# The first stage reordered: modulation by column groups, input weights in four transfers, half of the projection begun behind the first group

## The reference

```python
def rms_norm(x, g):
    return x * rsqrt(mean(x*x, -1) + 1e-6) * g
def modulate(x, g, shift, scale):
    return rms_norm(x, g) * (1 + scale) + shift

m  = silu(c)     @ w_mod + b_mod          # [1, 6*1024]; w_mod is [1024, 6144]
mc = silu(c_ctx) @ w_mod + b_mod
sh1, sc1, g1, sh2, sc2, g2 = split(m, 6)  # columns 0:1024 shift, 1024:2048 scale, ...
hx = modulate(x,   norm_attn_pre, sh1, sc1)
hc = modulate(ctx, norm_attn_pre, csh1, csc1)   # from mc
px = hx @ w_in                            # w_in is [1024, 960]
pc = hc @ w_in
# then: latent norms, query/key/value projections, rotation, attention of x over x and ctx,
# a Fourier mixing of part of px, w_out, the gated residual with g1,
# and a mixture of 32 experts, 4 for each token, over modulate(x, norm_ffn_pre, sh2, sc2).
# The second block (two layers of other attention kinds, each with an MLP) follows.
```

## Time and profile before

| | us |
|---|---|
| median of 3 runs | 1879.67 |
| lowest, highest | 1878.62, 1880.48 |
| span of the profiled execution, from first to last instruction | 1877.3 |

### The profile page before, as it was taken

How to read it: one execution, slowest core, us unless ns; L and a number is a source line. 1 busy time by engine, 2 the same in 40 slices (tenths; PEclk the granted TensorE clock), 3 DMA queues, 4 the chain that set the end, 5 groups by cost and what they waited for, 6 DMA issues and landing times. The chain is left out here.

```text
span 1877.3 us, 21793 instructions
## 1 busy us (share of the span) xinstructions
PE 1824.7 (97%) x8661; PEld 998.6 (53%) x8662; DVE 505.1 (27%) x1093; ACT 348.3 (19%) x688; POOL 10.9 (1%) x14
## 2 busy tenths in 40 slices
PE   6999899999999999999999999999999999999998
PEld 5757533333333333333333336768885466788743
DVE  1754411111011111011111104542025443211355
ACT  3221411111111111111111113332000032220001
POOL 0000000000000000000000000000000000000001
PEclk9999899999999999999999999999999999999999
DMA  9986599999999999999999999423355443134252
GB/s 401 324 184 276 207 416 430 431 432 432 431 431 431 433 431 431 431 431 432 431 431 430 432 429 328 155 105 105 135 176 177 146 174 135 45 135 158 86 170 102
DMA packets 101218, 558.43 MB, mean 297 GB/s; under 512 B 16936, under 2 KB 33805, under 8 KB 74413
## 3 DMA queue, kind: packets, MB, share of 16 engines
q1 hardware_dynamic: 98612, 553.06, 72.4%
q10 hardware_dynamic: 2554, 4.63, 1.9%
HBM read 552.43 MB, written 5.23 MB: 297 GB/s over the span
## 5 line engine op out<-in xcount | busy, mean ns | idle before, releaser
L1362 PE MATMUL ps<-ring,xs 128*64 128x512 f32 x2112 | 466.9, 593 | 8.5 <-DMA ring<-in_w_up 4.7
L1362 PEld LDWEIGHTS ps<-ring,xs 128*64 128x64 f32 x2112 | 151.1, 137 | 312.7 <-issue 293.9
L1416 PE MATMUL ps<-ring,actT 128*64 128x512 f32 x1056 | 233.9, 595 | 0.0
L2149 PE MATMUL ps<-hT,ring 128*128 128x256 f32 x1024 | 222.0, 379 | 0.2 <-ACT hT L1614 0.2
L2149 PEld LDWEIGHTS ps<-hT,ring 128*128 128x128 f32 x1024 | 194.3, 190 | 27.0 <-ACT hT L1614 0.6
L2174 PE MATMUL ps<-ring 128*128 128x512 f32 x448 | 192.8, 592 | 0.0
L1416 PEld LDWEIGHTS ps<-ring,actT 128*64 128x64 f32 x1056 | 73.1, 137 | 158.5 <-issue 131.7
L1489 DVE TENSOR_SCALAR hT<-ps 128x512 f32<-128x512 f32 x33 | 22.8, 692 | 448.0 <-PE ps L1362 448.0
L2174 PEld LDWEIGHTS ps<-ring 128*128 128x128 f32 x448 | 85.0, 190 | 105.8 <-issue 105.7
L1937 PE MATMUL ps<-hT,ring 128*128 128x256 f32 x512 | 117.9, 383 | 4.3 <-ACT hT L1614 2.9
L1937 PEld LDWEIGHTS ps<-hT,ring 128*128 128x128 f32 x512 | 94.7, 190 | 23.2 <-issue 5.9
(11 more groups left out here) (434 smaller groups left out, 1548.1 us busy)
## 6 DMA issues: line engine op xcount, KB each, us to landing
ring<-in_w_up SPq DMA_DIRECT2D x64, 2048.0 KB, 23.2
ring<-in_w_down SPq DMA_DIRECT2D x64, 2048.0 KB, 24.2
ring<-in_w_gate SPq DMA_DIRECT2D x64, 2048.0 KB, 22.7
ring<-in_mlp_w SPq DMA_DIRECT2D x16, 2048.0 KB, 7.7
ring<-in_mlp_w SPq DMA_DIRECT2D x32, 1024.0 KB, 5.3
ring<-in_w_mod SPq DMA_DIRECT2D x8, 2048.0 KB, 15.4
ring<-in_odd_w_in SPq DMA_DIRECT2D x6, 2048.0 KB, 7.7
ring<-in_w_mod SPq DMA_DIRECT2D x8, 1024.0 KB, 14.1
```

The costliest lines, as they stand in the source:

```text
L1362: mm = pe.matmul(ps[SLOTS * half:SLOTS * (half + 1), bank, :], xs[:, c % 4, c // 4 * SLOTS:(c // 4 + 1) * SLOTS], weights(v, 8 * part + c) ...
L1416: mm = pe.matmul(ps[SLOTS * half:SLOTS * (half + 1), Y, :], actT[:, f % 4, f // 4 * SLOTS:(f // 4 + 1) * SLOTS], weights(v, 16 + f)[:, hal ...
L2149: mm = pe.matmul(ps[:, bank + f // 2, (f % 2) * SEQ:(f % 2 + 1) * SEQ], mlp_w1[layer][g % 2][:, c, f * P:(f + 1) * P], hT[:, c, :], start= ...
```

## The change

- The first part of `w_mod` is split by column group: group g holds columns 512g to 512g+511 of shift and of scale. Each group is loaded by eight transfers (a chunk each, half a MiB, rows of 2 KB), into ring rows 0 to 7 and 8 to 15.
- `w_in` is loaded in four quarters, two behind each group's transfers.
- TensorE turns x first, into banks 4 to 7, then the small vectors, then `xn` into banks 0 to 3, now also behind `cols_ready`. The modulation runs group by group: four strips of 256 columns. Group 0 comes ahead of the projection, group 1 in the midst of it: its matmuls ahead of chunk 3's products, its transposes behind four of these.
- VectorE adds the bias and makes the gain for each group, chunks 0 to 3 for group 0, 4 to 7 for group 1, and so makes its four `hT` chunks behind group 1. ScalarE copies each group's bank on its own.
- SyncE's wait ahead of the second parts, and GpSimd's ahead of the clearing of `acc`, are for the second group now.

The diff, cut to its core:

```diff
+    moda = [ring[:, 8 * g:8 * g + 8, :].rearrange("p c (s n) -> p c s n", s=2) for g in range(2)]
...
-    win_in = [m.sem(f"win_in{k}") for k in range(2)]
+    win_in = [m.sem(f"win_in{k}") for k in range(4)]
...
-            pool.wait_ge(mods_ps, 1)
+            pool.wait_ge(mods_ps, 2)
             pool.memset(acc, 0.0).then_inc(zeroed, 1)
...
             sp.dma_start(x[:], stack(t["x"][0])).then_inc(x_in, 16)
-            for c in range(C):
-                sp.dma_start(ring[:, 2 * c:2 * c + 2, :].rearrange("p a n -> p (a n)"),
-                             t["w_mod"][0, c * P:(c + 1) * P, 0:2 * D]).then_inc(moda_in[c], 16)
-            for i in range(2):
-                src = stack(t["w_in"][0, 512 * i:512 * i + 512, :])
-                sp.dma_start(win[:, 4 * i:4 * i + 4, 0:IN_W], src).then_inc(win_in[i], 16)
-                sp.dma_start(win[:, 4 * i:4 * i + 4, IN_W:D], src[:, :, IN_W - ROPE:IN_W]).then_inc(win_in[i], 16)
+            halves = t["w_mod"][0].rearrange("(c p) (s n) -> p c s n", p=P, n=D)
+            for g in range(2):
+                for q in range(4):
+                    for k in range(2):
+                        c = 2 * q + k
+                        sp.dma_start(moda[g][:, c, :, :], halves[:, c, 0:2, 512 * g:512 * g + 512]).then_inc(moda_in[4 * g + q], 16)
+                for q in (2 * g, 2 * g + 1):
+                    src = stack(t["w_in"][0, 256 * q:256 * q + 256, :])
+                    sp.dma_start(win[:, 2 * q:2 * q + 2, 0:IN_W], src).then_inc(win_in[q], 16)
+                    sp.dma_start(win[:, 2 * q:2 * q + 2, IN_W:D], src[:, :, IN_W - ROPE:IN_W]).then_inc(win_in[q], 16)
             sp.dma_start(ctx_sb, stack(t["ctx"][0])).then_inc(ctx_in, 16)
...
-            sp.wait_ge(moda_ps, 1)
+            sp.wait_ge(moda_ps, 2)
             for c in range(3):
                 second_part(c)
...
             pe.wait_ge(consts_in, 16)
+            pe.wait_ge(x_in, 16)
+            turned(x, 4)
             pe.wait_ge(rows_in, 16 * len(ROWS))
-            pe.transpose(ps[:, 7, 0:NROWS], rows[0:NROWS, :], ident[0:NROWS, 0:NROWS]).then_inc(rows_t, 1)
-            pe.wait_ge(x_in, 16)
-            turned(x, 0)
+            pe.transpose(ps[:, 0, 0:NROWS], rows[0:NROWS, :], ident[0:NROWS, 0:NROWS]).then_inc(rows_t, 1)
             pe.wait_ge(normed, QT)
+            pe.wait_ge(cols_ready, 1)
+            turned(xn, 0)
+
+            def modulation(g, bank):
+
+                for c in range(C):
+                    if c % 2 == 0:
+                        pe.wait_ge(moda_in[4 * g + c // 2], 32)
+                    for j in range(4):
+                        mm = pe.matmul(ps[32 * j:32 * (j + 1), bank, 0:SEQ], silu32[:, c, :],
+                                       moda[g][:, c, j // 2, (j % 2) * SEQ:(j % 2 + 1) * SEQ], start=(c == 0), stop=(c == C - 1))
+                mm.then_inc(mods_ps, 1)
+
+            def modulation_turned(g, bank):
+                pe.wait_ge(mods_sb, g + 1)
+                for b in range(2):
+                    mm = pe.transpose(ps[:, bank, b * P:(b + 1) * P], mods[:, g * SEQ + b * P:g * SEQ + (b + 1) * P], ident)
+                mm.then_inc(moda_ps, 1)
+
+            pe.wait_ge(silu_ready, 2)
             pe.wait_ge(copied_a, 2)
             pe.wait_ge(copied_v, 2)
-            turned(xn, 0)
-
-            pe.wait_ge(silu_ready, 2)
-            for c in range(C):
-                pe.wait_ge(moda_in[c], 16)
-                for j in range(4):
-                    mm = pe.matmul(ps[32 * j:32 * (j + 1), 5, :], silu32[:, c, :],
-                                   ring[:, 2 * c + j // 2, (j % 2) * 512:(j % 2 + 1) * 512], start=(c == 0), stop=(c == C - 1))
-            mm.then_inc(mods_ps, 1)
-            pe.wait_ge(mods_sb, 1)
-            pe.wait_ge(cols_ready, 1)
-            for b in range(4):
-                mm = pe.transpose(ps[:, 7, b * P:(b + 1) * P], mods[:, b * P:(b + 1) * P], ident)
-            mm.then_inc(moda_ps, 1)
+            modulation(0, 5)
+            modulation_turned(0, 7)
...
-            keep_busy(m, pe, 5, 6)
-            pe.wait_ge(modv_ready, 4)
+            keep_busy(m, pe, 5, 3)
+            pe.wait_ge(modv_ready, 2)
             for c in range(C):
...
-                if c % 4 == 0:
-                    pe.wait_ge(win_in[c // 4], 32)
+                if c % 2 == 0:
+                    pe.wait_ge(win_in[c // 2], 32)
+                if c == 3:
+                    modulation(1, 0)
...
                 for n in range(8):
+                    if c == 3 and n == 4:
+                        modulation_turned(1, 1)
                     mm = product(4 + n // 2, n % 2, c, AT[n], hT)
...
             act.wait_ge(mods_ps, 1)
-            act.copy(mods, ps[:, 5, :]).then_inc(mods_sb, 1)
+            act.copy(mods[:, 0:SEQ], ps[:, 5, 0:SEQ]).then_inc(mods_sb, 1)
...
             modulated(hT, 0, 0)
+            act.wait_ge(mods_ps, 2)
+            act.copy(mods[:, SEQ:2 * SEQ], ps[:, 0, 0:SEQ]).then_inc(mods_sb, 1)
             act.wait_ge(ctx_in, 16)
...
+            def modulation(g, bank):
+                v.wait_ge(moda_ps, g + 1)
+                v.wait_ge(cols_ready, 1)
+                parts = modv[:].rearrange("p (s g h b) t -> p s g h b t", s=2, g=2, h=2)
+                bias = col(m, "bmod", 0, 16).rearrange("p (s g h b a) -> p s g h b a", s=2, g=2, h=2, a=1)
+                for b in range(2):
+                    raw = ps[:, bank, b * P:(b + 1) * P].rearrange("p (s h t) -> p s h t", s=2, h=2)[:, :, :, 0:2]
+                    v.tensor_tensor(parts[:, :, g, :, b, :], raw, bias[:, :, g, :, b, :].to_broadcast([P, 2, 2, 2]), ALU.add).then_inc(modv_ready, 1)
+                v.wait_ge(modv_ready, 2 * g + 2)
+                v.scalar_tensor_tensor(gain[:, 4 * g:4 * g + 4, :], modv[:, 8 + 4 * g:12 + 4 * g, :], 1.0, spread(col(m, "pre", 4 * g, 4), 2),
+                                       ALU.add, ALU.mult).then_inc(gain_ready, 1)
+
+            modulation(0, 7)
...
-            v.wait_ge(gain_ready, 1)
+            modulation(1, 1)
+            v.wait_ge(gain_ready, 2)
             v.wait_ge(x_ps, 2)
             modulated(hT, 0, 0)
```

More of the change, by code:

```diff
@@ L771, in _ @@
             for k in range(2):
-                act.copy(xT[:, 2 * k:2 * k + 2, :].rearrange("p a n -> p (a n)"), ps[:, k, :]).then_inc(copied_a, 1)
+                act.copy(xT[:, 2 * k:2 * k + 2, :].rearrange("p a n -> p (a n)"), ps[:, 4 + k, :]).then_inc(copied_a, 1)
             act.wait_ge(cols_ready, 1)
@@ L807, in q @@
                 return latent(bank, half, qlatT[:, k, :], sq_q[:, k, :], col(m, "qlat", k))
+            act.wait_ge(gain_ready, 2)
             act.wait_ge(x_ps, 3)
@@ L949, in _ @@
             v.memset(m.eps[:, 1:2], EPS2).then_inc(m.init, 1)
-            v.wait_ge(rows_t, 1)
-            v.tensor_copy(m.cols[:], ps[:, 7, 0:NROWS]).then_inc(cols_ready, 1)
             def normalize(dst, src, j):
@@ L960, in _ @@
             normalize(xn, x, 0)
+            v.wait_ge(rows_t, 1)
+            v.tensor_copy(m.cols[:], ps[:, 0, 0:NROWS]).then_inc(cols_ready, 1)
             v.wait_ge(x_ps, 1)
             for k in range(2, 4):
[L963 to L971, removed]
+                v.tensor_copy(xT[:, 2 * k:2 * k + 2, :].rearrange("p a n -> p (a n)"), ps[:, 4 + k, :]).then_inc(copied_v, 1)
+            def modulation(g, bank):
[10 more added lines that the diff above has]
+            modulation(0, 7)
             def modulated(dst, bank, which):
```

## The result

The change makes the kernel slower by 4.2 us: 1883.66 us median (1882.40 to 1885.09, 15 runs) against 1879.47 (1877.02 to 1880.48, 15 runs) taken beside it, a ratio of 1.0024 with a 95% interval of 1.0017 to 1.0032. A second time, beside the experiments, it was 1883.29 against 1878.92: 1.0020, 1.0011 to 1.0030. The profiled execution's span went from 1877.3 to 1882.9.

A forecast was written before the change was run, and what follows sets the result against it. It took the transfer queue as first bound, then two nearly equal chains at 64 us: TensorE's, and second parts, b_mod, adds, hcT. Late flow 2.6 plus clock 1.7 gave +4.3, on 1879.67: 1884.0 us, range 1880.2 to 1888.0.

The forecast's parts named there:

- The shift passes to the end: From the expert passes on: a shift of the first stage moves products and transfers alike and passes undiminished to the end.
- Rival (e): Expert stage: expert loads keep their time and TensorE's 8.5 us of waits shrink by the shift; 1879.7 us, chance 0.08.
- TensorE's gain: x products: they begin at 22.1 instead of 32.41 and end at 55.7, 6.5 us earlier than before.
- rival (b): Modulation: group 0 runs at the low pace, 3.5 us more before the products; +7.8, 1887.5 us, chance 0.10.
- The second parts late: SyncE's queue: second parts wait for group 1 until 38.4, flow resumes at 40.3 against 37.7, 2.6 us later.
- GpSimd's clearing: Clearing of acc: moves to the second group (39.6) but ends before SyncE has issued its three second parts (3.46 us).
- b_mod in order: Transfer queue: b_mod keeps its place behind 6.3 MB of second parts and lands at 56.5, 2.6 us later.
- Rival (d): Transfer queue: b_mod doesn't queue, landing some 4 us after its issue at 42; -7.4, 1872.3 us, chance 0.08.
- The clock: Behind TensorE's 9 us idle gap before the context products: 3.4 us at half pace, 1.7 us lost.
- Rival (a): First stage: the clock stays up or TensorE comes 1 to 2 us earlier; +1.0 to +2.8, say 1881.5, chance 0.22.
- The small pieces: Modulation loads: 8.39 MB in 2 KB pieces run at 409 GB/s, costing 0.9 us.
- Rival (c): Modulation loads: half-size transfers are slow, 315 GB/s, and the queue never stands empty; 6.9 + 1.7, 1888.3 us, chance 0.04.

The follow-up runs named there:

- e1: The changed kernel with VectorE making its half of hcT ahead of the first eight modulation adds; 1872.58 us against 1878.88 for the kernel before.
- e4: The kernel before, with SyncE issuing the second parts only after TensorE's second chunk of x products; 1883.34 us against 1878.88.
- e10: The changed kernel itself timed once more, beside e11 on the same chip; 1883.29 us against 1878.92 for the kernel before.
- e11: The changed kernel with the edits of e2 and e3 together, 16 idle matmuls in the gap; 1880.31 us against 1878.92 for the kernel before.
- e2: The changed kernel with the first two second parts issued behind group 0's wait, not group 1's; 1881.72 us against 1878.88 for the kernel before.
- e3: The changed kernel with 19 idle matmuls in TensorE's gap ahead of the context's fifth chunk; 1882.12 us against 1878.88 for the kernel before.
- e9: e8 with VectorE's two copies out of the projection banks also ahead of the eight adds; 1874.34 us against 1878.46 for the kernel before.
- e5: The kernel before, with the first modulation part loaded in sixteen half-MiB transfers by column group; 1880.04 us against 1878.46.
- e8: e1 with the first two second parts issued behind group 0 and b_mod ahead of the third; 1871.57 us against 1878.46 for the kernel before.
- e6: The kernel before, with VectorE making its half of hcT ahead of the eight modulation adds; 1878.60 us against 1878.46.

## Why the prediction was right

The forecast was 1884.0, +4.3; measured were 1883.66, +4.2. The likeliest case came about by its mechanism. That the total fits so closely is in part luck: at the up projections, where the mechanism ends, the loss was 6.4 us, half as much again as forecast. By its steps:

- **The shift passes to the end.** Right: 1648.2 and 1648.5 us behind the first pass, and 1647.5 to 1648.2 in e1 to e4, e10 and e11. Rival (e) fell.
- **TensorE's gain.** Right in kind: 6.5 us were forecast; in the change itself it is 4.94 (57.29 for 62.23), and in e1, where nothing covers it, 6.07. The start of the products was 1.3 us late (23.39 for 22.1), since group 0 ran 4.77 us instead of 3.5. Group 1, at the later pace, took 3.66. In e2, e3 and e9 group 0 took 3.66 as well: the early part of the kernel meets the change of pace at different points. This is a small piece of rival (b).
- **The second parts late.** Right in mechanism, 1.2 us too small in size. Issued at 39.76, not 38.4, b_mod +3.80 instead of +2.6; the cause is group 0 again. (The terms that the forecast gives, 37.8 and 0.3, make 38.1 and not 38.4; the step from group 1's end to the issue took what the 38.4 allowed.) In e1 and e3, where the issue came at 38.63 and 38.50, b_mod let the adds begin at 56.28 and 56.47, against the 56.5 of the forecast. e4 shows that this wait alone makes the loss, e2 that a full queue takes most of it away (2.84 of the 3.80; the rest is the price of the pieces).
- **GpSimd's clearing.** Forecast to end ahead of SyncE's three issues, which were taken as 3.46 us. With an empty queue they took 1.29 us, to 41.05; the clearing ended at 41.19, and b_mod was issued behind it at 41.22. That is under 0.2 us, and e4 has the whole loss without it.
- **b_mod in order.** It had the place in time that the forecast gave it: in every profile in which VectorE waited for it, the wait ended within 0.9 us of the third second part's landing, after it in the change (16.4 us behind its issue), e1, e3 and e10, and ahead of it in the kernel before, e2, e4, e5 and e11. Rival (d) fell. The prediction didn't see that its premise could be made true by an edit; e8 issues b_mod ahead of the third part.
- **The clock.** Right in mechanism, too small: 2.6 us for 1.7 (67.95 to 84.09 is 16.1 us, 65.09 to 78.61 in e11 is 13.5). I took the low clock to last 3.4 us, from the earlier trace rows. That is about what e4 shows behind its gap of 3.25 us, but in the change the clock was low from 67.95 until within the stretch 72 to 74, some 5.5 us of work. The trace of the kernel before had a warning that I passed over: granted clocks of 0.65, 0.50, 0.50 and 0.65 in the four stretches of 2 us from 218 to 226, together 6.8 us at the lower level. Rival (a) had called this term doubtful; e3 and e11 show it at the up mark.
- **The small pieces.** 0.9 us forecast, 0.98 in e5. Rival (c) fell, and for this kernel the rule of the Trainium skill that it leans on ("DMA: Bandwidth & Descriptors", section Bandwidth: at least 1 MiB for 75% of peak, 341 GB/s for 1 MB): half a MiB with rows of 2 KB, queued back to back, ran at 407 in e5.
- **Not foreseen:** 1.1 us less between the marks (151.4 to 150.3), where the clock of the routing part differs. So 3.8 + 2.6 - 1.1 = 5.3 at the first pass, and 5.6 in the span. The rest of the way to 4.2 is the scatter of single executions: the two that were profiled lay 1.1 us above and, by the estimate given with the result, 0.4 us below their medians. The forecast also put 2.4 us around the span, where the recorded executions have 1.8; the difference was the scatter of the profiled one. So two terms that were too small, by 1.2 and 0.9 us, were offset by differences that the forecast didn't know of.

## What to carry to other kernels

Before an engine's work is pulled ahead, find the second chain of nearly the same length; here two chains met within a microsecond, and one waited behind the other's buffers. When a buffer is read in parts, release and refill it in the same parts: a wait for the last of them stops everything queued behind it. And put what another engine waits for ahead of work that has all its time; the order that cost nothing before (e6) was worth some 11 us once the change had moved the chains (e1 against the change).

## What the runs showed of the hardware

- Behind the gap of 3.25 us in e4 the clock fell as well, and only after the work had resumed at 67.59: the granted clock is 1.00 in 66 to 68, then 0.68 and 0.50. These are its rows:

```profile
66.00:68.00 2.00, 0.41 (x2) 0.30 (x2) 2.00 (x4) 0.00 (x0) 0.00 (x0) 1.00 0.97 343
68.00:70.00 2.00, 2.00 (x8) 1.48 (x7) 2.00 (x5) 0.68 (x2) 0.00 (x0) 0.68 1.05 423
70.00:72.00 2.00, 2.00 (x6) 1.53 (x6) 2.00 (x2) 0.07 (x1) 0.00 (x0) 0.50 0.99 406
```

- The gap of 8.7 us cost 2.6 us behind it and that of 3.25 us cost 1.66. With filler matmuls through the gap the granted clock stayed at 1.00 from 56 to 74 (e3), and TensorE resumed 0.60 us behind hcT's start, as without them (0.59 in the change).
- The clock column reads 1.00 over 10 to 20 us in the kernel after, although sixteen transposes at 12.93 take 3.65 us there and 1.91 at 51.65. Here the durations told the pace, and the column didn't.
- Four strips of 32 output partitions took half the time with half the columns: 64 instructions in 3.66 us with 256 columns (group 1 in the change), against 7.07 with 512.
